# Squares behind features, the order at the sweep's ends, and unread products ahead of the first norm

## What is computed

```
for l in range(DEPTH):                       # DEPTH = 2
    mod = c_act @ w_mod[l] + b_mod[l]
    shift, scale, gate = jnp.split(mod[:, None, :], 3, axis=-1)
    h = rms_norm(x, g_pre[l]) * (1.0 + scale) + shift
    if l % 2 == 0:
        (gq, gk, gv, ga_f, ga_b, gz, cq, ckv, kr, mz) = _split(h @ w_in_e[e], EVEN_SPLITS)
        o_a = gla_branch(...)                # gated linear attention, two directions, chunks
        o_b = mla_branch(...)                # latent attention: 4 heads, softmax over 2048 keys
        y = jnp.concatenate([o_a, o_b], axis=-1) @ w_out_e[e]
    else:
        y = sgmlp_branch(...) @ w_out_o[o]   # gMLP over chunks of 128 tokens
    x = x + gate * rms_norm(y, g_post[l])
```

## Time and profile before

| | us |
|---|---|
| median of 3 runs (3111.93 to 3114.3) | 3113.76 |
| profiled execution, its own time | 3112.22 |
| its span | 3110.4 |
| TensorE busy | 2987.3 (96%) |
| VectorE, ScalarE, GpSimd busy | 1397.7, 1163.2, 691.0 |
| share of the chain that ended last: PE, issue, DVE, POOL, ACT, DMA | 85%, 4%, 4%, 3%, 3%, 1% |

### The profile page before, as it was taken

How to read it: one execution, slowest core, us unless ns; L and a number is a source line. 1 busy time by engine, 2 the same in 40 slices (tenths; PEclk the granted TensorE clock), 3 DMA queues, 4 the chain that set the end, 5 groups by cost and what they waited for, 6 DMA issues and landing times.

```text
span 3110.4 us, 46939 instructions
## 1 busy us (share of the span) xinstructions
PE 2987.3 (96%) x16548; PEld 2488.4 (80%) x16548; DVE 1397.7 (45%) x2513; ACT 1163.2 (37%) x2094; POOL 691.0 (22%) x722
## 2 busy tenths in 40 slices
PE   4899999999899999998999999999999999999999
PEld 3668888788688888886878888888888888877887
DVE  5467777855677777773343111122222222222011
ACT  4552245554455555552244111232332332322111
POOL 0121111266233333332320001012111211123221
PEclk8999999999999999999999999999999999999999
DMA  7132355596211221114542211211211211134231
GB/s 263 53 120 99 107 162 161 175 281 184 70 54 54 59 59 57 55 51 145 185 166 99 95 74 47 75 61 61 81 61 61 81 61 61 63 133 166 85 108 54
DMA packets 259931, 317.63 MB, mean 102 GB/s; under 512 B 17189, under 2 KB 187301, under 8 KB 257224
## 3 DMA queue, kind: packets, MB, share of 16 engines
q1 hardware_dynamic: 259816, 316.10, 31.0%
HBM read 213.67 MB, written 102.37 MB: 102 GB/s over the span
## 4 chain that ended last, share of the span: by engine, by line
PE 85%; issue 4%; DVE 4%; POOL 3%; ACT 3%; DMA 1%; SPq 0%; DVEq 0%; POOLq 0%; ACTq 0%
PE PS L342 12%; PE PS L344 11%; PE PS L343 11%; PE PS L2300 4%; PE PS L2302 4%; PE PS L2301 4%; PE PS L1769 4%; PE PS L2451 4%; PE PS L2453 4%; PE PS L2452 4%; PE PS L1748 3%; PE PS L1737 2%; PE PS L1770 2%; PE PS L1738 2%; PE PS L1739 2%
## 5 line engine op out<-in xcount | busy, mean ns | idle before, releaser
L342 PE MATMUL PS<-hTh,whi 128*128 128x512 f32 x1664 | 661.3, 397 | 21.6 <-DVE hTl L296 9.8
L343 PE MATMUL PS<-hTl,whi 128*128 128x512 f32 x1664 | 652.1, 392 | 0.0
L344 PE MATMUL PS<-hTh,wlo 128*128 128x512 f32 x1664 | 651.9, 392 | 0.0
L342 PEld LDWEIGHTS PS<-hTh,whi 128*128 128x128 f32 x1664 | 315.1, 189 | 96.5 <-DVE hTl L296 12.2
L344 PEld LDWEIGHTS PS<-hTh,wlo 128*128 128x128 f32 x1664 | 314.9, 189 | 66.8
L343 PEld LDWEIGHTS PS<-hTl,whi 128*128 128x128 f32 x1664 | 315.2, 189 | 63.5 <-issue 0.2
L332 POOL TENSOR_TENSOR whi<-wraw,zero 128x1024 fp32r<-128x1024 f32 x50 | 95.6, 1912 | 1181.0 <-PE PS L344 951.5
L1839 ACT ACTIVATE pb__167<-PS,nm,rq 128x512 f32<-128x512 f32 x256 | 197.1, 779 | 97.8 <-DVE nm L1902 97.2
L2300 PE MATMUL PS<-ow_h,of_h 128*128 128x512 f32 x576 | 225.4, 391 | 7.8 <-DVE oy L2255 7.8
L2301 PE MATMUL PS<-ow_l,of_h 128*128 128x512 f32 x576 | 224.9, 390 | 0.0
L2302 PE MATMUL PS<-ow_h,of_l 128*128 128x512 f32 x576 | 224.8, 390 | 0.0
(11 more groups left out here) (271 smaller groups left out, 5600.9 us busy)
## 6 DMA issues: line engine op xcount, KB each, us to landing
projT<-pev SPq DMA_DIRECT2D x80, 256.0 KB, 2.6
xt<-x SPq DMA_DIRECT2D x8, 2048.0 KB, 8.6
mw<-wmod SPq DMA_DIRECT2D x64, 256.0 KB, 2.8
oxt<-x SPq DMA_DIRECT2D x32, 512.0 KB, 4.6
sg_v<-vev SPq DMA_DIRECT2D x64, 256.0 KB, 2.4
wraw<-wuz SPq DMA_DIRECT2D x32, 512.0 KB, 5.4
vm<-sg_v SPq DMA_DIRECT2D x16, 1024.0 KB, 5.5
sgT<-mT SPq DMA_DIRECT2D x16, 1024.0 KB, 4.4
```

What stands on the lines that cost most here:

```text
L342: pe.matmul(PS[:, bank, :], w[1][:, s, k, :], hTh[:, k, b], start=(k == 0), stop=False)
L343: pe.matmul(PS[:, bank, :], w[1][:, s, k, :], hTl[:, k, b], start=False, stop=False)
L344: mm = pe.matmul(PS[:, bank, :], w[2][:, s, k, :], hTh[:, k, b], start=False, stop=(k == KD - 1))
```

## The change

Six edits.

1. `mod_pe` runs 44 products of ones by ones (`keep_busy`), as soon as 13 of the 16 partial sums are in and ahead of the second half's sums; `start_pe` runs 22 more behind `mod_pe`. They write a part of bank 1 that nothing reads.
2. `start_act` puts the squares of group g + 1 behind all 8 features of group g.
3. `norm_pool_front` and `norm_dve_scale` go by pairs of tiles instead of fours (in both layers).
4. The split of tile 2 waits for `s_pb` 15 (block 6) instead of 16 (block 7).
5. At the sweep's start the transposes of tile 1's keys stand ahead of the fold, and their copy ahead of the fold's evictions. At its end latent part 1 stands ahead of the last spread.
6. The attention's first scores wait for the last tile but one alone; pieces 0 and 1 come behind bank 0's scores, and only bank 1's scores wait for the last tile.

```diff
--- before.py
+++ after.py
@@ -180,9 +180,17 @@
                 mm = pe.matmul(PS[:, 0, j:j + 1], acc[:, k * P:(k + 1) * P], ones[:, 0:1], start=True, stop=True)
             return mm
 
+        def keep_busy(pe, n):
+            both = ones[:, :].bitcast(F32R)
+            for _ in range(n):
+                pe.matmul(PS[:, 1, 0:P], both, both, start=True, stop=True)
+
         def mod_pe(pe):
             pe.wait_ge(s_set, 1)
             for half in range(2):
+                if half:
+                    pe.wait_ge(s_macc, 2 * KD - 3)
+                    keep_busy(pe, 44)
                 pe.wait_ge(s_macc, KD * (half + 1))
                 mm = mod_cols(pe, macc0[:, half, 0:D], half)
             mm.then_inc(s_mps, 1)
@@ -264,16 +272,18 @@
                 act.activation(hTh[:, k, b], nt(l)[:, m % 4, :], ACT.Copy).then_inc(s_hh, 1)
 
         def norm_pool_front(pool, g):
-            c = slice(32 + 4 * (g % 2), 36 + 4 * (g % 2))
-            r = slice(40 + 4 * (g % 2), 44 + 4 * (g % 2))
-            pool.wait_ge(s_sq, 4 * (g + 1))
-            pool.tensor_scalar(small[:, r], small[:, c], 1.0 / D, EPS, ALU.mult, ALU.add).then_inc(s_rs, 1)
-            pool.wait_ge(s_rs, 2 * g + 1)
-            pool.tensor_tensor(small[:, r], small[:, r], negh[:, 0:4], ALU.pow).then_inc(s_rs, 1)
+            for p in range(2):
+                c = slice(32 + 4 * (g % 2) + 2 * p, 34 + 4 * (g % 2) + 2 * p)
+                r = slice(40 + 4 * (g % 2) + 2 * p, 42 + 4 * (g % 2) + 2 * p)
+                pool.wait_ge(s_sq, 4 * g + 2 * p + 2)
+                pool.tensor_scalar(small[:, r], small[:, c], 1.0 / D, EPS, ALU.mult, ALU.add).then_inc(s_rs, 1)
+                pool.wait_ge(s_rs, 4 * g + 2 * p + 1)
+                pool.tensor_tensor(small[:, r], small[:, r], negh[:, 0:2], ALU.pow).then_inc(s_rs, 1)
 
         def norm_dve_scale(dve, g):
-            dve.wait_ge(s_rs, 2 * g + 2)
             for t in range(4):
+                if t % 2 == 0:
+                    dve.wait_ge(s_rs, 4 * g + t + 2)
                 r = 40 + 4 * (g % 2) + t
                 dve.tensor_scalar(x_tile(g, t), x_tile(g, t), small[:, r:r + 1], None, ALU.mult).then_inc(s_xn, 1)
 
@@ -328,7 +338,7 @@
             hi = w[1][:, s, :, :].rearrange("p k c -> p (k c)")
             lo = w[2][:, s, :, :].rearrange("p k c -> p (k c)")
             pool.wait_ge(s_wr[s], (h + 1) * 16)
-            pool.wait_ge(s_pb, 16 if isinstance(g, int) and g == 2 else 4 * g + 4)
+            pool.wait_ge(s_pb, 15 if isinstance(g, int) and g == 2 else 4 * g + 4)
             pool.tensor_tensor(hi, w[0][:, s, :], zero[:, 0:1].broadcast_to([P, D]), ALU.add).then_inc(s_whi, 1)
             pool.wait_ge(s_whi, g + 1)
             pool.tensor_tensor(lo, w[0][:, s, :], hi.bitcast(F32), ALU.subtract).then_inc(s_wlo, 1)
@@ -419,8 +429,8 @@
                 proj_evict(act, 2 * g - 1)
                 for k in range(8):
                     norm_act(act, 8 * g + k)
-                    if k == 3 and g < 3:
-                        norm_act_front(act, g + 1)
+                if g < 3:
+                    norm_act_front(act, g + 1)
             proj_evict(act, 6)
             proj_evict(act, 7)
 
@@ -452,6 +462,7 @@
             for m in range(6):
                 norm_pe(pe, m)
             mod_pe(pe)
+            keep_busy(pe, 22)
             for m in range(6, 8):
                 norm_pe(pe, m)
             for j in range(8):
@@ -1126,6 +1137,7 @@
             act.wait_ge(s_wqr, E_wqr + 16)
             for k in range(2):
                 act.activation(wqh[:, k, 512:], wq[:, k, :], ACT.Identity, bias=zero[:, 0:1], scale=mcol[:, 3 + k:4 + k]).then_inc(s_pwh, 1)
+            main_turned(act, 1)
             for k in range(2):
                 act.wait_ge(s_fold, E_fold + k + 1)
                 act.activation(wqh[:, k, 0:512], PS[:, 3 + 2 * k, :], ACT.Identity, bias=zero[:, 0:1], scale=mcol[:, 3 + k:4 + k]
@@ -1435,7 +1447,7 @@
                     act.wait_ge(s_mog, t)
                 act.activation(orr[:, :], PS[:, n_bank(t), :], ACT.Copy).then_inc(s_mor, 1)
             for t in range(NT + 2):
-                if 0 < t < NT:
+                if 1 < t < NT:
                     main_turned(act, t)
                 if t == 0:
                     for y in range(NU - 2, NU):
@@ -1603,12 +1615,16 @@
                 if t < NT:
                     outputs(t)
                 if t == 0:
+                    turn(1)
                     fold_pe(pe)
-                if t + 1 < NT:
+                if t + 1 < NT and t:
                     turn(t + 1)
+                if t == NT:
+                    lat_pe(pe, t, 1)
                 if t:
                     spread(t - 1)
-                lat_pe(pe, t, 1)
+                if t < NT:
+                    lat_pe(pe, t, 1)
 
 
         mvh = at("mvh", M0, [P, MH, S], F32R)
@@ -1790,7 +1806,15 @@
                         if opening:
                             for n in ns:
                                 piece_pe(pe, n)
-                    scores(h, N, u, (0, 1))
+                    if opening and u == 0:
+                        pe.wait_ge(s_mog, NT - 1)
+                        scores(h, N, u, (0,))
+                        pieces(0, 1)
+                        pe.wait_ge(s_mog, NT)
+                        pe.wait_ge(s_mor, NT)
+                        scores(h, N, u, (1,))
+                    else:
+                        scores(h, N, u, (0, 1))
                     turn_if(0)
                     turn_if(1)
                     if u:
@@ -1804,7 +1828,7 @@
                         turn_if(3)
                         values_if(0)
                         values_if(1)
-                        pieces(*range(8))
+                        pieces(*range(2, 8))
                     else:
                         if not opening:
                             shares(I - 1)
@@ -1816,8 +1840,6 @@
                         pieces(14, 15)
                 if opening:
                     pe.wait_ge(s_kl, NT)
-            pe.wait_ge(s_mog, NT)
-            pe.wait_ge(s_mor, NT)
             pe.wait_ge(s_qa, 4 * NB)
             pe.wait_ge(s_qd, 6 * NB)
             pe.wait_ge(s_plo, 2 * NB)
```

## The result

| kernel | median of the runs, us | lowest to highest | ratio to before, 95% interval |
|---|---|---|---|
| before | 3113.74 | 3111.93 to 3114.30 | |
| changed | 3094.79 | 3091.59 to 3098.31 | 0.9940, 0.9923 to 0.9958 |

The account below looks back on a forecast made before the run. TensorE works nearly all the span, so gains come from its standstills and lower-clock stretches. Terms 0.7 + 1.5 + 11.4 + 5.0 + 3.0 + 6.3 = 27.9 off 3112.22 give 3084.3, plus 1.5 to the median 3085.8; range 3079 to 3094.

Parts of the forecast that it names:

- Modulation, +0.7 forecast: Modulation's partial sums: unread products raise the clock, so the second L180 group takes 1.84 us instead of 3.57; 0.7 us gained.
- work of this shape raises the clock before 24 of it are through: Modulation: inferred from 24 early transposes; 22 unread products then run at 0.21 us each, the other 22 at 0.12.
- rival (a): Modulation: unread products leave the clock down, group 1 begins near 69.4, gain 20.9 us, time 3092.8; chance 0.12.
- Group 1's start, 1.5: First norm: powers and scalings in pairs, TensorE's own products ending at 63.1; group 1's transposes gain 1.5 us.
- the case that the clock doesn't come: First norm, group 1's start: without the upper clock only 0.5 us is gained instead of 1.5.
- Groups 1 and 2, 11.4: First norm: without squares in their middle, 16.5 us a group, 33.0 instead of 44.4 for two; 11.4 us gained.
- Third tile, 5.0: Third weight tile's split: its wait is hidden, but L511 then waits for `ga`; 5.0 us gained, not 6.4.
- Sweep's start, 3.0: Sweep's start: latent sums begin 1.5 us earlier and 14 more records run at the upper clock; 3.0 us gained.
- I let it fall at the same moment: Sweep's start: the clock falls when it did before, after 24 instead of 10 records at the upper clock.
- Sweep's end, 6.3: Sweep's end: latent products fill idle time, last product near 791.0 instead of 797.1; 6.3 us, 3.0 if the clock falls.
- Second norm, 0: Second norm: eight more small GpSimd instructions under the output projection cost zero; uncovered, 1 us a group.
- Signs: What would show the forecast, from modulation to sweep's end: L180's time, group spacing, waits, contribution 1's start, scores at clock 1.00.

Follow-up runs that it names:

- the 44 alone: Changed kernel without the 22 unread products behind the sums, the 44 kept: 3094.79 us, ratio to before 0.9938.
- wide or half-width ones: Changed kernel with unread products of 128x512 (16 and 8) or 128x256 (28 and 16) for the 44 and 22: 3087.45 and 3088.76 us.
- `ga` ahead of the store: Changed kernel with the gate loads, `ga` among them, issued ahead of the store of block 7's result: 3090.73 us, ratio to before 0.9928.

## Why the prediction was wrong, point by point

**Modulation, +0.7 forecast: wrong, and it decides.** The step that failed is "work of this shape raises the clock before 24 of it are through". The 24 transposes did raise it; the narrow fp32r products did not, in 44, 16 sums and 22 more. The rival (a) had this, with 0.12, and its times are met: 44 ended at 46.9 (46.5), the sums at 50.2 (50.1), the 22 at 55.0 (54.7). Only block 0 was kinder: three products at the low pace instead of nine, group 1 at 67.99 instead of 69.4. In place of 0.7 + 1.5 stands -3.3: 5.5 of the 7.3 us by which the profiled time was missed. The price at the lower clock, 0.21, was right (0.219). That (a)'s total of 20.9 meets the 20.6 of the traces so closely is luck: it kept the other terms at 25.7, they came to 23.9, and block 0 gave 1.4 back.
**Group 1's start, 1.5.** Hidden under the loss above. Without unread products group 1 begins 1.2 earlier than before, 0.7 of which was there already at the second sums: 0.5, the value named for the case that the clock doesn't come. With unread transposes, where it does come, group 1 begins 3.3 earlier, above the 2.2 of both terms.
**Groups 1 and 2, 11.4.** Right: 11.5. The chain was right: the power over two columns took 0.69 (0.75 assumed) and the two scalings 1.42 (1.4). Only the parting was not: the prediction names the squares' place as the cause and shows the pairs' share in the power alone (16.8 with one of 1.02), while the scalings of the first pair are the larger part of it.
**Third tile, 5.0.** Right at the gate product (5.2), with `ga` as the next wait (1.1). What failed is that the start of L511 was taken as the point that counts, with nothing said of the clock behind it: the new standstill let the clock fall behind it, -1.5. That isn't fixed: it happened in the changed kernel, with the 44 alone, with unread transposes and with the third tile's edit alone, and didn't without unread products or with wide or half-width ones, where TensorE stood 1.1 to 1.4 us all the same.
**Sweep's start, 3.0.** The moved waits were right to 0.1 us. The term of the clock, "I let it fall at the same moment", 14 x 0.11, failed: it fell 1.1 us behind the first sum, as before, and so 6.0 us behind the fold in place of 7.4. What is left is 1.4, near the 1.5 named as the low end.
**Sweep's end, 6.3.** The clock stayed at 1.00 through the scores, as said; 5.6 gained there, 5.2 kept, for the pieces then wait a microsecond longer. The prediction's own working ends at 6.1 (797.1 to 791.0), not 6.3.
**Second norm, 0.** Over the whole rest of the span 0.6 is lost. TensorE's waits in the second norm are no longer than before (5.5 us in all against 6.0 up to its second group of transposes), but 1.2 us go there to one more stretch at the lower clock:

```profile
1600.60:1604.00 3.40, 3.40 (x13) 2.83 (x14) 3.25 (x5) 3.16 (x5) 0.00 (x0) 0.50 0.10 8
```

All nine kernels with pairs in the second norm have this stretch, and so have two of the five without pairs (the third tile's edit and the sweep's start alone). So it isn't the pairs alone; whether they make it more likely stays open.
**What nobody had.** 1.7 us from the sweep's middle, where the work is the same: before the change TensorE ran at the lower clock there from 710.4 to 717.2 and from 754.8 to 758.2, afterwards only from 696.0 to 702.9. I count it as luck: the sweep's start alone shows the opposite sign. This also bounds what a single profile can say: from tile 2's transposes to the last sums it is 144.8 to 149.4 us in the kernels here, with the same work.
**Signs.** Groups 16.5 apart, no wait for `wlo`, 1 to 2 us ahead of the gate product, contribution 1 behind the state, scores within 1 us of the last spread at clock 1.00: all met. The first one, L180 in 1.9 us begun by 44.7, failed (3.51, at 46.68). Of the two things by which it was to be wrong most, the group pace above 18 us did not come, and the lower clock in the first 48 products did, for three of them.

## What to carry to other kernels

Before paying for unread work to keep TensorE's clock up, put the very instruction there and look at the granted clock: of two kinds that took the same 0.21 us each, one raised it and one didn't; against no unread work at all the wrong one cost 4.5 us at group 1 and the right one gained 2.1. Compare with the kernel that has none of it, and further on than the next wait: the 2.1 were gone at the fold, and no run here shows a total that unread work ahead of the first norm made better than leaving it out. Count a removed standstill only together with the next one: if TensorE still stops for a microsecond, the lower clock may only move to its other side. When squares, a power and scalings form a chain, cutting it in pairs saves the scalings of the first pair too.

## What the runs showed of the hardware that was not expected

- Unread fp32r products of 128x128, 66 of them with 16 one-column sums between (17.8 us without a gap), left the granted clock at 0.50. Transposes of 128x128 in fp32, begun at 36.67, had raised it by 40.3, and so did fp32r products over 256 columns (begun at 36.59, 41.8) and over 512 (38.40, 44.4).
- At the lower clock fp32r products over 128 and over 256 columns start the same 0.213 us apart, those over 512 columns 0.427.
- The Trainium skill, "TensorE: Matmul & The Clock Gate", section "Part 4: PE-mode transpose", says that transposes don't count as busy for the clock in the way that products do. For fp32 transposes the run with unread ones shows the opposite (0.50, then 0.93 with nothing else on TensorE, and 1.00 from 40.3 us on); the measurement decides.
- The granted clock is printed as 1.00 from the start of the span, but in the trace with `ga` ahead of the store the first transposes start 0.21 us apart until 26.2 us and 0.11 behind it, the paces of the lower and the upper level. For the first stretch of a trace the pace is the better witness.
- The same 16 unread products raised the clock at 44.4 us in one trace and at 41.8 in another (begun at 38.40 and 37.32). The Trainium skill, "TensorE: Matmul & The Clock Gate", section "What's actually happening", says that the rise comes at other moments from run to run; the traces agree.
- Runs of one kernel differ by 1.2 us (unread transposes) to 9.3 (3084.87 to 3094.16 without unread products; 3108.52 to 3117.30 of the kernel before), often more than a single term here. That the places of the lower clock make this spread is likely but not shown, for each kernel has one trace.
- GpSimd's power over 128x2 takes 0.69 us, over 128x4 1.01.
